# Returning expert outputs to tokens: a gated float32 table replaced by a zero/one table in two float32r passes

## What is computed

```python
# gate: (256 tokens, 64 experts), zero but for the 8 experts of each token
def expert_block(args):
    xb, gb = args
    a = jnp.einsum('td,edf->tef', xb, e_w1)      # 1024 -> 256
    b = jnp.einsum('td,edf->tef', xb, e_w3)
    act = jax.nn.silu(a) * b * gb.astype(xb.dtype)[..., None]
    return jnp.einsum('tef,efd->td', act, e_w2)  # 256 -> 1024
...
return h + routed + shared
```

## Time and profile before

| | |
|---|---|
| time, median of 3 runs | 599.57 us (599.1 to 600.29) |
| span of the profiled execution | 598.5 us |
| difference of the two | 1.07 us, outside the span |
| read from HBM | 222 MB, 373 GB/s over the span |
| TensorE busy | 576.6 us, 96% |
| VectorE, ScalarE busy | 237.2 us (40%), 152.0 us (25%) |

### The profile page before, as it was taken

How to read it: one execution, slowest core, us unless ns; L and a number is a source line. 1 busy time by engine, 2 the same in 40 slices (tenths; PEclk the granted TensorE clock), 3 DMA queues, 4 the chain that set the end, 5 groups by cost and what they waited for, 6 DMA issues and landing times.

```text
span 598.5 us, 10089 instructions
## 1 busy us (share of the span) xinstructions
PE 576.6 (96%) x4012; PEld 270.4 (45%) x4012; DVE 237.2 (40%) x622; ACT 152.0 (25%) x325; POOL 19.2 (3%) x66
## 2 busy tenths in 40 slices
PE   9999999999999998999979999999999999999686
PEld 6455566557343444453534434434343434344322
DVE  5999753468623423134121431314132332313122
ACT  6953763146120220211102102212121212020101
POOL 4001220000000000000000000000000000000000
PEclk9999999999999999999989999999999999999898
DMA  8973577995899999999999999999999999999995
GB/s 315 430 289 123 63 234 286 419 375 183 317 374 428 424 423 424 430 418 426 428 420 425 425 429 422 429 418 428 422 428 420 431 418 429 422 428 426 421 407 180
DMA packets 30975, 225.00 MB, mean 376 GB/s; under 512 B 6848, under 2 KB 7360, under 8 KB 12736
## 3 DMA queue, kind: packets, MB, share of 16 engines
q1 hardware_dynamic: 30208, 223.17, 91.2%
q10 hardware_dynamic: 720, 1.18, 0.6%
HBM read 222.11 MB, written 1.05 MB: 373 GB/s over the span
## 4 chain that ended last, share of the span: by engine, by line
PE 84%; DMA 12%; DVE 1%; issue 1%; ACT 1%; SPq 0%; DVEq 0%; ACTq 0%
PE bank L736 81%; DMA ring<-in_e_w 10%; DMA wreg<-in_e_w 2%; PE bank L1176 1%; PE bank L1203 1%; PE bank L783 0%; PE bank L974 0%; DVE wreg L1620 0%; PE bank L831 0%; ACT wreg L1335 0%; DVE wreg L1931 0%; SPq L369 0%; PE bank L804 0%; PE bank L941 0%; DVE reg_d L2082 0%
## 5 line engine op out<-in xcount | busy, mean ns | idle before, releaser
L736 PE MATMUL bank<-ring,wreg 128*32 128x512 f32 (+2 forms) x1256 | 257.4, 600 | 5.1 <-issue 3.3
L736 PE MATMUL bank<-wreg 128*32 128x512 f32 (+6 forms) x493 | 163.4, 586 | 0.6 <-DVE wreg L1620 0.3
L736 PEld LDWEIGHTS bank<-ring,wreg 128*32 128x32 f32 (+1 forms) x1256 | 71.9, 119 | 119.5 <-issue 116.7
L1620 DVE TENSOR_TENSOR wreg<-wreg,bank 128x256 f32<-128x256 f32 (+1 forms) x29 | 11.9, 412 | 170.8 <-ACT wreg L1525 163.7
L736 PE MATMUL bank<-wreg,reg_ab 128*128 128x512 f32 (+1 forms) x192 | 75.4, 543 | 0.0
L736 PE MATMUL bank<-reg_ab,wreg 128*32 128x512 f32 (+2 forms) x160 | 65.4, 563 | 1.4 <-DMA ring<-in_e_w 1.4
L736 PE MATMUL bank<-reg_d 128*128 128x512 f32 (+1 forms) x140 | 63.6, 593 | 2.9 <-DVE reg_d L2082 2.9
L1335 ACT ACTIVATE reg_d<-bank 128x512 f32<-128x512 f32 (+2 forms) x46 | 21.6, 470 | 163.5 <-PE bank L736 100.0
L736 PE MATMUL bank<-side,wreg 128*32 128x512 f32 (+2 forms) x142 | 57.5, 604 | 4.7 <-DMA ring<-in_e_w 4.7
L736 PEld LDWEIGHTS bank<-wreg 128*32 128x32 f32 (+4 forms) x493 | 47.7, 128 | 29.7 <-issue 28.1
L1620 DVE TENSOR_TENSOR acc<-acc,bank 128x512 f32<-128x512 f32 (+1 forms) x70 | 47.1, 673 | 30.4 <-PE bank L736 29.2
(11 more groups left out here) (211 smaller groups left out, 402.8 us busy)
## 6 DMA issues: line engine op xcount, KB each, us to landing
ring<-in_e_w SPq DMA_DIRECT2D x33, 2048.0 KB, 20.5
ring<-in_e_w SPq DMA_DIRECT2D x52, 1024.0 KB, 17.9
wreg<-in_e_w SPq DMA_DIRECT2D x12, 2048.0 KB, 20.4
wreg<-in_e_w SPq DMA_DIRECT2D x18, 1024.0 KB, 15.2
reg_ab<-in_e_w SPq DMA_DIRECT2D x7, 2048.0 KB, 22.8
side<-in_e_w SPq DMA_DIRECT2D x9, 1024.0 KB, 19.5
wreg<-in_w_in SPq DMA_DIRECT2D x2, 2048.0 KB, 25.2
wreg<-in_w_out SPq DMA_DIRECT2D x1, 4096.0 KB, 12.8
```

The source lines that it names most:

```text
L736: return nc.tensor.matmul(out_, lhsT, rhs, start=start, stop=stop, **kw)
L1620: return nc.vector.tensor_tensor(out_, a, b, op)
```

## The change

The gate is taken out of the table and applied to y.

- `PT` is now zero/one: `slots_out` on VectorE compares the transposed table with zero (`ts(..., ALU.not_equal)`), and a sum along its rows (`tensor_reduce`) gives the gate of each slot, `gate_col`. ScalarE has no part in it any more.
- y leaves PSUM in two steps for each bank: ScalarE writes `y_high` = gate times y, rounded to float32r; then VectorE writes `y_low` = gate times y minus `y_high`.
- `combine` multiplies `PT` with `y_high` and with `y_low`, two float32r matmuls into the same bank instead of one in float32.
- `y_split` (`y_high` and `y_low`) has room for one half only. So the second half (a = 1) of a plain batch is taken out of PSUM in the next batch, after the first half has been combined, and is combined after `up(it, 1)` (or `up_all`). `add_batch` becomes two calls of `add_half`, and `slots_out` is called once for each half.
- `down_done` becomes `y_bank_done`, which counts banks. SyncE waits at the same points as before, with doubled numbers.

```diff
-            def combine(it, kind, shared=False):
-
-                for a in range(2):
-                    pe.wait_ge(S["y_act"], it * 2 + (a + 1))
-                    pe.wait_ge(S["y_dve"], it * 2 + (a + 1))
-                    for hf in range(2):
-                        bank = ps[y_bank(a) + hf]
...
-                        mm(bank[:, :], PT[:, a, :], y_s[:, 0 if kind == "small" else a, 512 * hf:512 * hf + 512],
-                           not shared, True).then_inc(S["comb_mm"], 1)
+            def combine(it, kind, a, shared=False):
+
+                for hf in range(2):
+                    bank, w = ps[y_bank(a) + hf], slice(512 * hf, 512 * hf + 512)
+                    if kind != "small" or a == 0:
+                        pe.wait_ge(S["y_low_done"], it * 4 + (2 * hf + 2 if kind == "small" else 2 * a + hf + 1))
...
+                    mm(bank[:, :], PT[:, a, :], y_high[:, w], not shared, False)
+                    mm(bank[:, :], PT[:, a, :], y_low[:, w], False, True).then_inc(S["comb_mm"], 1)
...
                 else:
                     up(it, 0, before, kind, loads)
-                    combine(before, was, shared)
-                    turn_slots(it, kind)
+                    combine(before, was, 0, shared)
+                    if was == "small":
+                        combine(before, was, 1, shared)
+                    turn_slots(it)
                     up(it, 1, before, kind, loads)
+                    if was != "small":
+                        combine(before, was, 1, shared)
...
+                    pe.wait_ge(S["PT_ready"], it * 2 + 1)
                     gather_slices(0, small, next_sh)
+                    pe.wait_ge(S["PT_ready"], it * 2 + 2)
                     gather_slices(1, small, next_sh)
...
             def y_out(it, a, by=1):
 
-                dve.wait_ge(S["down_done"], it * 2 + (a + 1))
-                nc.vector.tensor_copy(y_s[:, a, 512:1024], ps[y_bank(a) + 1][:, :]).then_inc(S["y_dve"], by)
...
+                for hf in range(2):
+                    w = slice(512 * hf, 512 * hf + 512)
+                    dve.wait_ge(S["y_high_done"], it * 4 + (2 * a + (hf + 1) * by))
+                    stt(y_low[:, w], ps[y_bank(a) + hf][:, :], gate_of(a, by), y_high[:, w].bitcast(FP32),
+                        ALU.mult, ALU.subtract).then_inc(S["y_low_done"], by)
...
             it = x_before + (N_LAST + 1)
+            for n, (c0, c1) in enumerate(LAST_COLUMNS):
+                dve.wait_ge(S["y_high_done"], it * 4 + (n + 1))
+                stt(y_low[:, c0:c1], ps[n % 2][:, 0:c1 - c0], gate_of(0, 2), y_high[:, c0:c1].bitcast(FP32),
+                    ALU.mult, ALU.subtract).then_inc(S["y_low_done"], 1)
             dve.wait_ge(S["acc_added"], it * 4)
             for n, (c0, c1) in enumerate(LAST_COLUMNS):
                 for a in range(2):
```

More of the change, by code:

```diff
@@ L8 @@
 FP32 = mybir.dt.float32
+FP32R = mybir.dt.float32r
 BF16 = mybir.dt.bfloat16
@@ L1545, in _, with batch @@
             copy(parts[1], rest).then_inc(S["parts_copied"], 1)
-            def slots_out(it):
-                act.wait_ge(S["gt_done"], it * 2 + 1)
-                copy(PT[:, 0, :], ps[6][:, 0:128]).then_inc(S["gm_act"], 1)
-            def batch(it, kind="plain", then="plain", sh=None, next_sh=None):
+            def batch(it, kind="plain", was="plain", then="plain", sh=None, next_sh=None):
                 by = 2 if kind == "small" else 1
                 if kind == "small":
-                    slots_out(it)
+                    if was != "small":
+                        y_out(it - 1, 1)
                     silu(it, 0, by)
@@ L1597, in _ @@
             for it in range(1, N_FIRST):
-                batch(it, FIRST_BATCHES[it], FIRST_BATCHES[it + 1] if it + 1 < N_FIRST else "plain", beside(it), beside(it + 1))
+                batch(it, FIRST_BATCHES[it], FIRST_BATCHES[it - 1], FIRST_BATCHES[it + 1] if it + 1 < N_FIRST else "plain",
+                      beside(it), beside(it + 1))
             with act.Fori(N_FIRST, x_before + 1) as it:
@@ L1601, in _ @@
             batch(x_before + 1, then="small")
-            with act.Fori(2, N_LAST + 1) as s:
-                batch(x_before + s, "small", "small")
-            batch(x_before + (N_LAST + 1), "small", None)
+            batch(x_before + N_LAST, "small", then="small")
+            batch(x_before + (N_LAST + 1), "small", "small", None)
             act.wait_ge(S["acc_added"], (x_before + (N_LAST + 1)) * 4 + 6)
@@ new lines, in _, with slots_out @@
+            n_small = [0]
+            def slots_out(it, a, kind="plain"):
+                dve.wait_ge(S["gt_done"], it * 2 + (a + 1))
+                turned = ps[6 + a][:, 0:128]
+                ts(PT[:, a], turned, 0.0, ALU.not_equal)
+                last = nc.vector.tensor_reduce(gate_col[:, a:a + 1], turned, AX.X, ALU.add)
+                if kind == "small" and a == 1:
+                    last.then_inc(S["gates_turned"], 1)
+                    n_small[0] += 1
+                    dve.wait_ge(S["gates_turned"], n_small[0])
+                    last = tt(gate_col[:, 2:3], gate_col[:, 0:1], gate_col[:, 1:2], ALU.add)
+                last.then_inc(S["PT_ready"], 1)
@@ L2094, in add_batch, with add_half, batch @@
+            def add_half(it, a):
+                if a == 0 and not (isinstance(it, int) and it == 0):
+                    dve.wait_ge(S["acc_added"], it * 4)
+                for c in (2 * a, 2 * a + 1):
+                    dve.wait_ge(S["comb_mm"], it * 4 + (c + 1))
                     part = acc[:, 512 * c:512 * c + 512]
                     tt(part, part, ps[2 + c][:, :], ALU.add).then_inc(S["acc_added"], 1)
-            def batch(before, kind="plain", then="plain", at=None, sh=None, next_sh=None):
-                it = 0 if before is None else before + 1
+            def batch(before, kind="plain", was="plain", then="plain", at=None, sh=None, next_sh=None):
+                it = before + 1
@@ L2113, in batch @@
                     activate(it, 0, by)
+                if was != "small":
+                    add_half(before, 1)
+                    slots_out(it, 1, kind)
                 if sh is not None:
```

145 lines of the change are left out of this document (76 added, 69 removed).

## The result

The changed kernel takes 602.0 us (median, 601.03 to 603.58), the kernel before, in the same comparison, 600.62 us (599.1 to 603.0). The ratio is 1.0022 with a 95% interval of [1.0013, 1.0031]: 1.3 to 1.4 us slower. The forecast was 0.85 us slower than before, at 600.4 us in a range of 598.5 to 602.5. The range held the time. Of the 1.6 us between 602.0 and 600.4, 1.05 us are the kernel before itself, whose median is 600.62 here and was 599.57 in the three runs that the forecast started from; the other 0.5 us are what the change costs beyond the 0.85.

A forecast was written before the change was run, and what follows sets the result against it. The prediction took the DMA stream of weights as the bound, so only start and tail count: span 598.5 + 0 (start) + 0 (stream) + 0.85 (tail) = 599.35, plus 1.07 to the median, 600.4 us; range 598.5 to 602.5.

The forecast's parts named there:

- The starting point: Whole kernel: profiled span 598.5 us, plus 1.07 us between span and median.
- The start: Load at 176.64 us, waiting for the first batch's `down`: unchanged; 0.9 us if the `PT` operations were not covered.
- The price of a pass: Combine matmuls: a float32r pass of 512 columns takes 0.213 us, saving 27 us of TensorE work over 16 batches.
- The stalls: Second gather waiting for `PT` in ten batches: 1.1 to 1.7 us each, 11 to 17 us together.
- rival 1: Whole kernel: TensorE sets the time, so 13 us are saved, giving 586.6 us; chance 7%.
- The stream holds: Weight stream, 179 to 585 us: DMA never runs empty, saved passes become waits for weights, gain 0.
- The two narrow places: Loads at 205.07 and 215.93 us: 2.6 and 1.6 us of queued DMA work left when the next room is freed.
- The tail: Behind the last weights: six additions queue after the last remainder, 3.12 us, ending at 596.0; +0.85 us.
- rival 2: Last VectorE queue: dearer passes (from 0.30 us), closer outputs or a slow clock make it slower, 601.4 us; chance 29%.
- Rival 2's other half: Tail, 586.4 to 590.0 us: low clock lasts until the third `down` ends, +1.6 us, 602.0 us; within rival 2's share.
- a pass as dear as float32: Combine matmuls: a float32r pass costs 0.853 us, giving about 650 us; chance 4%.
- Rival 4: Tail: does not queue, TensorE's savings count and VectorE's work does not, -1.1 us, 598.3 us; chance 6%.

The follow-up runs named there:

- half of the first weights: Each whole 2 MB load of e_w1 and e_w3 cut to its first 1 MB: kernel before 584.41 us (0.9726), changed kernel 569.89 us (0.9482).
- the kernel with one pass: Changed kernel without the `y_low` product in the body, last batch keeping both passes: 602.09 us against 600.67, ratio 1.0023.
- the kernel with four: Changed kernel with both float32r products of each bank issued twice in the body, except the shared expert's batch: 601.96 us against 600.35, ratio 1.0021.
- variant with the late output: Kernel before with its first output transfer waiting for the fourth addition instead of the second: 601.75 us against 600.67, ratio 1.0017.
- The kernel with the old tail under the new body: Changed kernel with the last batch as in the kernel before (float32 table and y, one product, no remainder): 600.39 us against 600.35, ratio 0.9993.
- the reordered kernel: Changed kernel with VectorE adding the first piece before making the third remainder: 599.8 us (0.9987), and 599.97 us (0.999) when run again.

## Why the prediction came out as it did

**The starting point: 0.7 us too low.** The forecast added 1.07 us "between span and median", the difference of the profiled span, 598.5, and the median of three runs, 599.57. But in the 20 runs of the changed kernel the time is 1.7 to 1.9 us above the span of the same run, and the same holds for all later runs of the kernel before. So the profiled execution was by all signs the slowest of the three, 600.29 us, and 599.35 us of span would have meant about 601.1. What is then left to 602.0 is about as large as the output term below. That 602.0 lies within the range is in part luck: its upper end, 602.5, was set by a dearer pass and a lasting slow clock, and the measured median needed neither. (The chances named for "slower", 29, 4 and 9, make 42% and not 40.)

**What bounds the kernel: right.** The DMA share of 1.01, not TensorE's 96%, was the reading that decided, and the two runs with less and more passes bear it out over 34 us of TensorE's load. With half of the first weights the kernel before falls only to 584.4 us: TensorE's own bound lies 16 us under the time, so both readings of the page were near each other, and the DMA share told them apart.

**The start: right.** The loads that were issued at 176.64 are issued at 176.86. This is within what two executions differ by.

**The price of a pass: near.** Four passes over 512 columns, two banks of a plain batch:

```profile
409.94 1.21 PE L745 MATMUL bank<-y_split,PT 128*128 128x512 f32 x4
...
410.81 1.28 DVE L1639 TENSOR_TENSOR acc<-acc,bank 128x512 f32<-128x512 f32 x2
411.00 0.39 PE L1185 MATMUL bank<-ident,wreg 128*128 128x128 f32 x2
...
412.01 0.28 DVE L1642 TENSOR_SCALAR PT<-bank 128x128 fp32r<-128x128 f32 x1
412.21 0.28 DVE L2113 TENSOR_REDUCE small<-bank 128x1 f32<-128x128 f32 x1
412.55 0.84 PE L745 MATMUL bank<-side,reg_c 128*128 128x128 bf16 x12 [0.49 <-DVE small L2113]
```

A group of two, four and eight passes takes 0.57, 1.06 and 1.98 us to the transposes behind it (411.89 to 412.46 in the kernel with one pass, the rows above, and 412.89 to 414.87 in the kernel with four), so one pass more costs 0.23 to 0.25 us, and a group some 0.1 us besides. (The busy time of TensorE as a whole gives less, 10.5 us for 64 passes and 23.2 for 120, but it does not compare like with like: the mean granted clock of these three executions is 0.967, 0.984 and 0.991.) The cheap end of the bounds, 0.213, was thus close to the right one. But from the first pass to the transposes (409.94 to 411.00) it is 1.06 us, not 0.85, so a batch of two such groups saves 3.54 - 2.12 = 1.4 us and not 1.7 (3.54 is from 403.31 to the transposes of that batch, the row below). Over 16 batches that is 23 us, not 27; with half of the first weights, where both kernels have nearly the full clock (0.999 and 0.996), TensorE's busy time falls by the same 23 us (570.2 to 547.2).

```profile
406.85 0.38 PE L1203 MATMUL bank<-ident,side 128*128 128x128 f32 x2
```

**The stalls: right place, too large.** In the same rows the additions of a batch are back to back, 1.28 us for two instead of the 1.48 that was taken, and the two operations for `PT` are 0.20 apart instead of 0.3. The second gather waits 0.49 us, where 1.1 was predicted; in three other batches it is up to 1.4. The waits that the forecast summed to 11 to 17 us are 3.0 + 2.8 = 5.8 us; in all, waits for VectorE grew by 6.2 us (9.1 - 2.9). With half of the first weights the sum can be set against a measurement: 23 us of passes, less 6.9 us of waits for VectorE (9.8 - 2.9), less about 1.4 us for the tail if it costs the same there, is 14.7 us, and 14.5 were measured. The two errors of the prediction, passes too good and stalls too bad, had the same size, so that rival 1's 13 us came out near the 14.5 as well.

**The stream holds: right.** From 195 to 220 us the DMA share is 1.02 in both kernels. The two narrow places got wider. The `up_done` loads are issued at 192.37 instead of 194.65, and the two that had little in hand at 204.39 instead of 205.07 and 212.76 instead of 215.93:

```profile
192.37 0.33 SPq L378 DMA_DIRECT2D reg_ab<-in_e_w  x1
...
204.39 0.33 SPq L381 DMA_DIRECT2D side<-in_e_w  x1
...
212.76 0.85 SPq L378 DMA_DIRECT2D ring<-in_e_w  x2
```

**The tail: the mechanism was right, one term was taken as nothing.** The forecast said that all six additions queue behind the last remainder, and they do. Counted from the first `down` of the last batch, they end 9.69 us later (585.57 to 595.26), in 2.60 us and not 3.12. In the profile of the kernel before it was 9.77 us (585.38 to 595.15), no less, because that execution had a granted clock of 0.53 in this stretch and this one 1.00. The third `down` starts at 590.62 as predicted (590.7), but for another reason: it waits for its own weights, which land then (the forecast had them there already), and not for the combine. (Where the clock was low, as in the second profile of the changed kernel, the combine came later and the weights were there.)

To have the kernel before at the same clock, its variant with the late output serves, whose additions are unchanged: 587.64 to 596.56, 8.92 us. So the queue costs 0.77 us, where +0.85 was forecast; between the two executions with a low clock, the profile before and the second one of the changed kernel (585.35 to 596.09, 10.74 us), it is 0.97. The step that failed is the sentence behind it: that the last output goes "and takes as long". From its issue to the end of the span it takes 4.1 instead of 3.3 us, +0.8 us: three outputs of SyncE now leave in 1.44 us instead of 2.66. The kernel before with its first output held back shows the same 4.2 us, with nothing else changed. The forecast saw the mechanism (rival 2 names "the output DMAs closer together") and priced it as a part of a surplus, from no row. It is as large as the term that was worked out. By rows at the full clock the tail is thus some 1.6 us longer; the medians say 1.3 to 1.4.

**The clock.** Rival 2's other half, a low clock that lasts longer behind a longer wait, did not come about in the profiled execution: the granted clock is 1.00 from 586.4 to 590.0, the full level of 2.4 GHz, where it was 0.53 before, although TensorE had waited longer just ahead of it, 1.57 us instead of 0.98. In the other profile of the changed kernel it is lower at the same place, the row from 587 us on:

```profile
587.00:590.00 3.00, 2.58 (x28) 0.85 (x20) 0.49 (x1) 1.04 (x2) 0.00 (x0) 0.78 0.44 167
```

Its tail, from the first `down` at 585.35 to 600.4, takes 15.05 us, against 13.9 at the full clock, and 13.1 in the profile of the kernel before. The kernel with the old tail under the new body had 0.60 in this stretch. The Trainium skill, "TensorE: Matmul & The Clock Gate", section HAM oscillation, ties such a start at half rate to waits for DMA between bursts; some of these traces show it and some do not, with waits of the same length (1.57 and 1.58 us; the waits in the page's example are longer), so it adds about 1 us to single executions of either kernel. How often each kernel meets it was not counted, so that a part of the loss by a low clock in more executions is not ruled out; a loss by the clock alone is, since the reordered kernel waits as long there (1.59 us) and shows none.

**The rivals.** TensorE as the bound (586.6 us) and a pass as dear as float32 (650 us) have fallen. Of rival 2 the stated condition, a pass above 0.30 us, is false; its surplus by outputs is what came. Rival 4, a tail that does not queue, is what the reordered kernel makes: 599.8 and 599.97 us, not the 598.3 that it named. That is some 1.9 us below the changed kernel and 0.4 to 0.9 us below the one before, but neither interval against the kernel before (up to 1.0 and to 1.0005) settles that it is faster.

## What to carry to other kernels

A busy share of 96% does not make TensorE the bound when the DMA share is 1 throughout, as here; cutting the bytes shows what a saving on the engine is worth (14.5 us here) and keeping them shows that none of it arrives. In a kernel that follows its weights only the start and the tail count: there, read each engine's queue in its order, and put work that is ready ahead of work that waits. Spread the outputs as well: here the last one landed 1.2 us later when others had left just ahead of it.

## What the runs showed of the hardware

Float32r matmuls of 512 columns cost 0.23 to 0.25 us a pass at 128 by 128 and full clock, against 0.85 us for a float32 matmul of the same columns. A group has some 0.1 us besides: two, four and eight passes take 0.57, 1.06 and 1.98 us to the next float32 instruction.

The records of VectorE's additions out of PSUM overlap when nothing stands between them: 2.60 us for two of 512 and four of 256 columns, where the single times (0.68 and 0.42 us) sum to 3.0 us.

Three SyncE outputs and one from ScalarE, issued within 1.4 us, are followed by the end of the span 4.1 to 4.2 us after the last issue from SyncE. With SyncE's three spread over 2.7 us it comes after 3.3 to 3.4 us, and after 3.6 us in the first run of the reordered kernel, where they are spread over 2.3. In the kernel with the late output, bunching and a last issue that waits 0.6 us together are 1.0 us of the median.
